# The first turn of a transformer step's first matrix product: scaled inputs in own buffers, squares and their sums moved

## The reference

```python
def _rms_norm(x, g):
    xf = x.astype(jnp.float32)
    y = xf * lax.rsqrt(jnp.mean(xf * xf, axis=-1, keepdims=True) + EPS)
    return (y * g.astype(jnp.float32)).astype(x.dtype)

def _swiglu(x, w_in, w_out):
    gate, up = jnp.split(x @ w_in, 2, axis=-1)
    return (jax.nn.silu(gate) * up) @ w_out
...
    for layer in range(DEPTH):
        h = h + 0.5 * _swiglu(_rms_norm(h, p['g_ffn'][layer, 0]), p['w_ffn_in'][layer, 0], p['w_ffn_out'][layer, 0])
        # attention (latent in layer 0, forgetting in layer 1), then a second SwiGLU block
```

## Time and profile before

| | us |
|---|---|
| median of 3 runs | 2300.83 |
| lowest, highest | 2297.99, 2303.32 |
| time of the profiled execution | 2304.47 |
| its span in the trace | 2302.7 |
| PE busy in it | 2245.8 (98%) |
| mean granted TensorE clock | 0.983 |

### The profile page before, as it was taken

One profiled execution on the slowest core, in us unless ns is written; L12 is line 12 of the kernel. 1 busy time (PEld: TensorE's weight loads), 2 busy tenths in 40 slices (PEclk: granted clock), 3 DMA queues, 4 the chain that ended last, 5 costly groups with the idle time before them and its releaser, 6 DMA issues.

```text
span 2302.7 us, 45753 instructions
## 1 busy us (share of the span) xinstructions
PE 2245.8 (98%) x16715; PEld 2163.0 (94%) x16715; DVE 1685.7 (73%) x2707; ACT 1081.3 (47%) x1829; POOL 308.3 (13%) x274
## 2 busy tenths in 40 slices
PE   8999999999999999999999999999989999999997
PEld 8999999988989999999987999999878899999997
DVE  7975984578886995896356984995357868966973
ACT  6532543456665652453224551453247756533531
POOL 0000002045542000001131000001134420000001
PEclk9999999999999999999999999999989999999998
DMA  3322322100002223222223222223212212322221
GB/s 114 110 94 80 110 102 90 47 25 21 10 27 84 76 93 114 79 104 97 72 84 116 100 100 100 91 97 106 74 38 55 58 64 74 109 88 88 108 94 64
DMA packets 72749, 187.56 MB, mean 81 GB/s; under 512 B 40724, under 2 KB 42212, under 8 KB 61384
## 3 DMA queue, kind: packets, MB, share of 16 engines
q1 hardware_dynamic: 71368, 181.73, 23.3%
q0 software_dynamic: 1280, 4.49, 0.5%
HBM read 178.75 MB, written 7.35 MB: 81 GB/s over the span
## 4 chain that ended last, share of the span: by engine, by line
PE 87%; DVE 6%; ACT 3%; issue 3%; POOL 1%; DVEq 0%; DMA 0%; ACTq 0%; SPq 0%; POOLq 0%
PE ps L708 21%; PE ps L650 19%; PE ps L651 18%; PE ps L652 18%; PE ps L811 6%; PE ps L1030 1%; PE ps L966 1%; DVE hid_lo L1929 1%; PE ps L1057 1%; PE ps L668 1%; DVE arena L2333 0%; DVE x_lo L1929 0%; DVE stat L2236 0%; DVE xs_lo L1929 0%; DVE w_lo L1919 0%
## 5 line engine op out<-in xcount | busy, mean ns | idle before, releaser
L650 PE MATMUL ps<-xs_hi,w_hi 128*128 128x272 f32 x1408 | 410.3, 291 | 1.8 <-DVE scratch L2031 1.8
L652 PE MATMUL ps<-xs_hi,w_lo 128*128 128x272 f32 x1408 | 408.1, 290 | 0.0
L651 PE MATMUL ps<-xs_lo,w_hi 128*128 128x272 f32 x1408 | 407.4, 289 | 0.0
L1333 ACT ACTIVATE w_hi<-raw 128x1408 fp32r<-128x1408 f32 (+4 forms) x123 | 146.0, 1188 | 477.3 <-PE ps L708 225.4
L1376 ACT ACTIVATE w_hi<-w_blocks 128x1024 fp32r<-128x1024 f32 x176 | 186.8, 1061 | 308.8 <-PE ps L652 155.9
L651 PE MATMUL ps<-xs_lo,w_hi_more 128*128 128x272 f32 x1056 | 306.1, 290 | 0.0
L650 PE MATMUL ps<-xs_hi,w_hi_more 128*128 128x272 f32 x1056 | 305.7, 289 | 0.0
L708 PE MATMUL ps<-hid_hi,w_hi 128*128 128x256 f32 (+1 forms) x1312 | 270.7, 287 | 1.3 <-DVE w_lo L1919 1.0
L708 PE MATMUL ps<-hid_lo,w_hi 128*128 128x256 f32 (+1 forms) x1312 | 269.7, 286 | 0.0
L708 PE MATMUL ps<-hid_hi,w_lo 128*128 128x256 f32 (+1 forms) x1312 | 269.6, 286 | 0.0
L650 PEld LDWEIGHTS ps<-xs_hi,w_hi 128*128 128x128 f32 x1408 | 266.7, 189 | 2.9 <-issue 2.0
(11 more groups left out here) (271 smaller groups left out, 5063.8 us busy)
## 6 DMA issues: line engine op xcount, KB each, us to landing
w_blocks<-w_ffn_in SPq DMA_DIRECT2D x88, 1024.0 KB, 4.8
raw<-w_ffn_out SPq DMA_DIRECT2D x64, 704.0 KB, 4.1
raw<-w_b_kv SPq DMA_DIRECT2D x16, 512.0 KB, 3.7
raw<-w_a_out SPq DMA_DIRECT2D x8, 512.0 KB, 3.8
raw<-w_b_q SPq DMA_DIRECT2D x8, 512.0 KB, 3.6
raw<-w_b_out SPq DMA_DIRECT2D x8, 512.0 KB, 3.6
raw<-w_a_in SPq DMA_DIRECT2D x4, 672.0 KB, 4.0
raw<-w_a_qup SPq DMA_DIRECT2D x8, 288.0 KB, 2.8
```

The costliest lines, as they stand in the source:

```text
L650: pe.matmul(out, lhs[0], rhs[0], start=start, stop=False, skip_group_check=more)
L651: pe.matmul(out, lhs[0], rhs[1], start=False, stop=False, skip_group_check=more)
L652: return pe.matmul(out, lhs[1], rhs[0], start=False, stop=stop, skip_group_check=more)
L1333: act.activation(wh[par][:, 0:n], raw[par][:, 0:n], ACT.Copy).then_inc(w_hi, 1)
```

## The change

- ACT issues, ahead of everything, an activation that reads the small constant `eps` and whose result is never used; the load of its function table stands with it.
- Each pair is scaled into a buffer of its own (`xts[k]`: pairs 0 and 3 the old one, pairs 1 and 2 two regions that hold hidden activations later); only pair 3 waits for `xb` of pair 0.
- ACT's two squares of a pair stand behind its two roundings; the wait for sums(k-1) moves from `scale_x` to `square`.
- On PE sums(1) moves from ahead of the products to behind product set 1, sums(2) behind product set 2, sums(3) behind product set 3; the 5 idle matmuls behind sums(1) go.
- The semaphore numbering follows the new order; SUPDATE, used by two later stages, keeps the old one.

```diff
--- before.py
+++ after.py
@@ -95,9 +95,9 @@
         return self.sem, self.base + i * len(self.names) + self.names.index(name) + 1
 
 
-XSPLIT = {"act": ["g0", "sq0", "g1", "sq1", "xa", "xb"], "dve": ["t1", "t2", "t3", "t4", "xa", "xb"],
+XSPLIT = {"act": ["g0", "g1", "xa", "xb", "sq0", "sq1"], "dve": ["t1", "t2", "t3", "t4", "xa", "xb"],
           "pe": ["ss0", "ss1"]}
-SUPDATE = {"act": XSPLIT["act"], "dve": ["h0", "t1", "h1", "t2", "t3", "t4", "xa", "xb"], "pool": ["acc0", "acc1"]}
+SUPDATE = {"act": ["g0", "sq0", "g1", "sq1", "xa", "xb"], "dve": ["h0", "t1", "h1", "t2", "t3", "t4", "xa", "xb"], "pool": ["acc0", "acc1"]}
 RESPLIT = {"act": ["g0", "g1", "xa", "xb"], "dve": ["t1", "t2", "t3", "t4"]}
 RELOW = {"dve": ["xa", "xb"]}
 UPDATE = {"dve": ["e", "h", "x_lo"], "act": ["x_hi", "sq"], "pool": ["acc"]}
@@ -724,16 +724,12 @@
                     if first and "pe" in x:
                         add_squares(x, q["rms"], 3, 0)
                         keep_clock(5, 8)
-                        add_squares(x, q["rms"], 3, 1)
-                        keep_clock(5, 5)
                     pe.wait_ge(*ws.at("01", i))
 
                     pe.wait_ge(*st["dve"].at("c21", i - 2))
                     if first:
                         pe.wait_ge(*ws.at("23", i))
                         for n, k in enumerate(q["order"]):
-                            if "pe" in x and n > 1:
-                                add_squares(x, q["rms"], 3, n)
                             if x in split_squares and n == DK - 1:
                                 end_squares(x, q["rms"], 3)
                             pe.wait_ge(*x["dve"].at("xa", n))
@@ -741,6 +737,8 @@
                                 mm = times(par, j, k)
                                 if n == DK - 1:
                                     mm.then_inc(st["pe"].sem, 1)
+                            if "pe" in x and n > 0:
+                                add_squares(x, q["rms"], 3, n)
                         if q["rms"] is not None and "pe" not in x and x not in split_squares:
                             sum_squares(x, q["rms"], 3)
                     else:
@@ -1383,8 +1381,6 @@
 
             def scale_x(x, k, e, j, gain, buf):
 
-                if "pe" in x:
-                    act.wait_ge(*x["pe"].at(f"ss{j}", e - 1))
                 if "pool" in x:
 
                     act.wait_ge(*x["pool"].at(f"acc{j}", e - 1))
@@ -1395,6 +1391,8 @@
 
             def square(x, k, e, j):
 
+                if "pe" in x:
+                    act.wait_ge(*x["pe"].at(f"ss{j}", e - 1))
                 act.activation(scratch[j], tile(h, k + DK * j), ACT.Square).then_inc(x["act"].sem, 1)
 
             def round_x(x, k, e, buf):
@@ -1501,14 +1499,18 @@
                     ffn_in(q) if q["kind"] == "in" else out_proj(q)
 
 
+            act.wait_ge(set_dve, 2)
+            act.activation(rtok[:, 0:1], eps[:, 0:1], ACT.Copy)
             act.wait_ge(loaded["gains"], 16)
             for k in range(DK):
                 act.wait_ge(loaded["x"][k], 16)
-                act.wait_ge(*X0["dve"].at("xb", k - 1))
+                if k == DK - 1:
+                    act.wait_ge(*X0["dve"].at("xb", 0))
                 for j in range(2):
-                    scale_x(X0, k, k, j, G_FFN, xt[:, :])
+                    scale_x(X0, k, k, j, G_FFN, xts[k])
+                round_x(X0, k, k, xts[k])
+                for j in range(2):
                     square(X0, k, k, j)
-                round_x(X0, k, k, xt[:, :])
                 if k == 0:
                     first_pair(F0[0], ["01"])
                 if k == 1:
@@ -2132,9 +2134,9 @@
             dve.memset(stat[:, :], 1.0).then_inc(set_dve, 1)
             dve.wait_ge(loaded["gains"], 16)
             for k in range(DK):
-                mix_x(X0, k, 0, xt[:, :])
-                mix_x(X0, k, 1, xt[:, :])
-                low_x(X0, k, k, xt[:, :])
+                mix_x(X0, k, 0, xts[k])
+                mix_x(X0, k, 1, xts[k])
+                low_x(X0, k, k, xts[k])
                 if k == 0:
                     first_sums(F0[0])
                     first_pair(F0[0], ["01"])
```

## The result

| us | before | changed |
|---|---|---|
| median of 9 runs each | 2303.32 | 2308.37 |
| lowest, highest | 2297.99, 2307.39 | 2302.75, 2314.99 |
| profiled execution, span | 2304.47, 2302.7 | 2303.12, 2301.3 |

The ratio of the changed kernel to the one before is 1.0027, 95% interval [1.0015, 1.0039]: slower, by 3.5 to 9.0 us, with 6.2 in the middle. The forecast, 4.7 us more than before and 2305.5 us in all, put the loss beneath that middle, and the time 2.9 us too low: 2.5 of these are the base, whose median was 2300.83 with 3 runs and 2303.32 with 9.

A forecast was written before the change was run, and what follows sets the result against it. PE was taken to bound the kernel (busy 98% of the span). The spread's loss, 6.2 us or 3.2 against an unlucky before, gave a middle of 4.7 on the 2300.83 us median: 2305.5 us, range 2300 to 2309.3.

The forecast's parts named there:

- The head: Stretch up to the first product: early table load and reordered ACT work start it at 20.9 instead of 23.03, 2.1 us won.
- The pause of PE: Between the idle matmuls behind sums(0) and the first product: PE pauses 2.9 us.
- The squares' new wait: ACT's squares of pair 2 wait for sums(1), running at 26.0 and 27.1; product set 3 starts 1.7 us later.
- Sums(3) uncovered: Between product set 3 and j = 3, nothing hides sums(3): 4.4 us at the low level, 2.3 at the high.
- The low level: PE's clock is at its lower level from product set 3 on: 6.2 us lost at the spread instead of 1.9.
- From j = 3 to the spread: 24 products before the norm factor's spread, 12 at the low clock and 12 at the high: 4.2 us, spread at 44.1.
- the full loss: Rival: before is lucky with its clock in the median run too; 6.2 to 7.5 us lost, 2307 to 2308.5; chance 0.2.
- Against which time: Choice of base for the first turn's loss: middle of 6.2 and 3.2, 4.7 us, on the median of 2300.83.
- the unlucky clock: In before's first turn the clock rises 2.9 us after the first product, not 1.3: before about 3 us slower, loss 3.2.
- the lucky end: Loss of 6.2 us if before's clock rises early, 1.3 us after the first product, as in its profiled execution.
- the clock stays high: Rival: clock high from 24.3 on; costs 1.9 us, or -1.1 with an unlucky before, middle 0.4: 2301.2 us; chance 0.2.
- the head decides: Rival: clock high from the first product to j = 3; 0.4 us slower than the profiled run or 2.6 faster; chance 0.06.

The follow-up runs named there:

- own scratch: The changed kernel with pair 1's squares in a scratch pair of their own, so pair 2's squares don't wait for sums(1): 2304.66 us, 1.0018 to before.
- sums(3) short: The changed kernel with the last pair's sums over one group of frames instead of five: 2303.28 us, ratio 1.0004 to before.
- PE's order back: The changed kernel with PE's old order of sums, products and 5 idle matmuls; ACT's new order, buffers and early table stay: 2303.54 us, 1.0009 to before.
- third profile: The kernel before, unchanged, profiled a third time: first product at 22.30 us, spread of the norm's factor at 39.69 us.
- pause filled: The changed kernel with 15 idle matmuls instead of 8 behind sums(0): 2307.92 us, ratio 1.0016 to before.

## Why the prediction came out as it did

- *The head*: forecast 2.1 us won at the first product (20.9); measured 1.6 to 1.9 (first product at 21.18 to 21.47) against the first profile of before, and 0.8 to 1.1 against the two in which before starts at 22.3. The input landed 0.3 us later than I read. The table load won 1.0 of the 1.29. Right.
- *The pause of PE* before the first product: forecast 2.9 us, measured 3.26. Right, and filling it gave back 1.7 us of the turn: it isn't the main cause of the loss.
- *The squares' new wait*: forecast until 26.0 and 27.1, measured 26.55 and 27.67; product set 3 forecast at 33.5, measured 34.04. Right; "own scratch" gives the wait 1.3 us of the 2.3 lost at set 3, PE's work the rest.
- *Sums(3) uncovered*: forecast 4.4 us at the low level, measured 4.26, and j = 3 at 40.37 for a forecast of 39.9. Right; shown by "sums(3) short" and "PE's order back".
- *The low level*: right in all three profiles of the changed kernel.
- *From j = 3 to the spread*: too small. I let the clock rise after 12 of the 24 products, as it had 2.9 us into the dense run of before; it stayed at a half for all 24 in two profiles and for all but the last three in the third: 5.6 us instead of 4.2. The spread was forecast at 44.1 and came at 45.4 to 46.6. This is the part that I had put into the rival "the full loss" and given 0.2.
- *Against which time*: the step "the loss is 6.2 where before is lucky and 3.2 where it isn't, I take the middle, 4.7" was wrong in both ends. Two of four profiles of before have the unlucky clock, so the case is there, but it costs them 1.7 us and not 3. My sum for the 3 didn't follow from its own premise: a rise 2.9 us after the first product is at 25.9, before the 18 products end, and leaves sums(2) at the high level, so it comes to some 0.7 us, not to 1.2 + 2.2. In the third profile the first product starts 0.7 us earlier (22.30), all 18 products are low (1.25 us more), sums(2) is still nearly high (2.35 us), sums(3) is low (1.6 us more up to set 3), and 0.5 us goes into the wait for the diagonals at the spread, which that profile doesn't have. With the measured numbers the two ends are 45.99 - 38.07 = 7.9 and 45.99 - 39.70 = 6.3, middle 7.1.

So the forecast chose the right side and the right mechanism, and sized the sum 1.5 us under the launch's middle (4.7 for 6.2) and 2.4 under the turn's own (7.1). Two terms failed. The larger is the run from j = 3 to the spread: 4.2 us forecast, 5.6 measured, which with set 3's 0.5 us makes the lucky end 7.9 for 6.2. The smaller is the discount for an unlucky clock in the kernel before: half of 3 us forecast, half of 1.6 measured, 0.7 us. Both are the clock's level in a stretch, which I had put at a moment taken from one other place in one profile. With that the forecast lay just at the bound of 0.2%, with a chance of 0.47 for no change, where the measured terms would have put it clearly beyond. That the launch came nearer to the forecast than the turn did is no merit of the sum. The rivals "the clock stays high" and "the head decides" are out; "pause filled" had the full clock over the first 18 products, as the second of them asks, and lost all the same, as the clock fell at 27.6. What makes the clock fall and rise where it does stays open, in the turn and behind 450 us alike, and so does whether the change touches the later falls; they move single runs by more than the change does.

## What to carry to other kernels

Work that only fills a wait should stay in front of the wait: moved behind it, it costs its full length, and here double, since it ran at the clock's lower level (4.26 us for 2.29). When a buffer's reader is moved later, look for its next writer and for what is queued behind that writer; the writer's in-order engine carries the delay to everyone. And where a start is won by moving work, count the place to which it goes before counting the start. And where single launches scatter by more than the change is worth, time the changed stretch itself in several profiles.

## What the runs showed of the hardware that was not expected

- The function table's load, issued on an engine that waited for nothing, took 1.28 us at 2.65 and the dependent activation followed at once (3.94): nothing lies between them. A later load of the kernel before, ahead of the square root, is the same:

```profile
33.37 0.38 ACT L1424 ACTIVATE scratch<-ps 128x272 f32<-128x272 f32 x1
33.76 1.28 ACT L1342 ACT_TABLE_LOAD   x1
```

  The activation before it ends at 33.75 and the root starts at 35.06. The Trainium skill, "ScalarE: Activation LUTs", section "What ACT_TABLE_LOAD costs", states about 1.28 us for the load and a drain of about 1.38 us with every switch to another set. The load agrees; no row here shows the drain.
- The 20 instructions of a block of sums (ten one-column matmuls in 32-bit floats) take 2.29 us at the high and 4.26 to 4.43 us at the low level, that is 0.11 and 0.21 to 0.22 us each, against 0.126 and 0.227 us for a product of 272 columns. So one such sum, two instructions, costs more than a product, though it yields one column.
- The granted clock in the windows reads 1.00 before the first recorded event, while the rows there show the low level (0.22 us for each instruction of sums(0) in every profile): before the first event the durations must be read instead.
- With 30 idle instructions (from 14.27) and a pause of 1.96 us the clock was full at the first product and stayed so for 6.3 us. With 16 and a pause of 3.26 us it was full for the first six products in one of three profiles and fell at 22.3; in the other two the products lasted 0.43 us, the low level's, from the second on.
